# A decoder trunk in one kernel: attention scores and values as products of high and low parts, a stacked rotary part, and buffers laid out anew

## What is computed

```python
# layer A: differential attention, 8 heads, two maps a head, head dim 128, values 256 wide
s1 = einsum(qa, k1) * 128**-0.5;  s2 = einsum(qb, k2) * 128**-0.5
a  = causal_softmax(s1) - lam * causal_softmax(s2)
o  = rms_norm(a @ v, subln_g) * (1 - lam_init)
x += o @ w_o
x += square(relu(rms_norm(x) @ w_up)) @ w_down            # d_ff = 8192
# shared latents and layer B: 16 heads, 128 plain + 64 rotary columns, values 128 wide
kv = rms_norm(rms_norm(x) @ w_dkv[:, :512]) @ w_ukv ;  k_rope = rope(rms_norm(x) @ w_dkv[:, 512:])
q  = rms_norm(rms_norm(x) @ w_dq) @ w_uq
s  = (einsum(q_nope, k_nope) + einsum(rope(q_rope), k_rope)) * 192**-0.5
x += (causal_softmax(s) @ v) @ w_o ;  x += square(relu(rms_norm(x) @ w_up)) @ w_down
return rms_norm(x, final_norm_g)
```

## Time and profile before

| | us |
|---|---|
| median of 3 runs | 2063.35 |
| the profiled execution | 2063.65 |
| its span, first to last instruction | 2061.9 |
| TensorE matmuls busy | 2051.7 (100%) |
| TensorE weight loads busy | 1761.2 (85%) |
| VectorE busy | 1194.4 (58%) |
| ScalarE busy | 989.3 (48%) |
| GpSimd busy | 10.1 (0%) |

### The profile page before, as it was taken

One profiled execution on the slowest core, in us unless ns is written; L12 is line 12 of the kernel. 1 busy time (PEld: TensorE's weight loads), 2 busy tenths in 40 slices (PEclk: granted clock), 3 DMA queues, 4 the chain that ended last, 5 costly groups with the idle time before them and its releaser, 6 DMA issues.

```text
span 2061.9 us, 28683 instructions
## 1 busy us (share of the span) xinstructions
PE 2051.7 (100%) x10470; PEld 1761.2 (85%) x10470; DVE 1194.4 (58%) x1474; ACT 989.3 (48%) x1360; POOL 10.1 (0%) x22
## 2 busy tenths in 40 slices
PE   9999999999999999999999999999999999999998
PEld 7888888888888888888888998888888888888887
DVE  7655555565556556555655666566556556655655
ACT  7554555444345334434446665544434434434443
POOL 0000000000000000000000000000000000000000
PEclk9999999999999999999999999999999999999999
DMA  7655545665665665556555444575666556656653
GB/s 278 239 164 169 177 161 166 190 196 186 194 193 176 207 187 184 202 183 190 196 184 164 136 131 146 187 218 184 198 190 183 200 186 183 202 187 181 203 186 120
DMA packets 261129, 381.76 MB, mean 185 GB/s; under 512 B 8785, under 2 KB 145233, under 8 KB 260945
## 3 DMA queue, kind: packets, MB, share of 16 engines
q1 hardware_dynamic: 260352, 378.90, 57.3%
q10 hardware_dynamic: 720, 2.10, 0.3%
HBM read 378.87 MB, written 2.10 MB: 185 GB/s over the span
## 4 chain that ended last, share of the span: by engine, by line
PE 84%; issue 15%; DVE 0%; POOL 0%; ACT 0%; POOLq 0%; DVEq 0%
PE acc L470 23%; PE acc L441 15%; PE acc L443 15%; PE acc L442 15%; PE acc L480 12%; PE side L505 1%; PE side L785 0%; PE side L784 0%; PE acc L751 0%; PE acc L759 0%; PE acc L760 0%; PE acc L761 0%; PE acc L752 0%; PE acc L753 0%; PE side L795 0%
## 5 line engine op out<-in xcount | busy, mean ns | idle before, releaser
L1289 DVE TENSOR_TENSOR wlo<-raw,whi 128x1024 fp32r<-128x1024 f32 (+1 forms) x700 | 840.3, 1213 | 663.5 <-ACT whi L879 661.7
L879 ACT ACTIVATE whi<-raw 128x1024 fp32r<-128x1024 f32 (+1 forms) x700 | 726.2, 1051 | 727.8 <-PE acc L443 479.4
L441 PE MATMUL acc<-whi,opB 128*128 128x512 f32 x1264 | 493.4, 390 | 0.0
L443 PE MATMUL acc<-whi,opB 128*128 128x512 f32 x1264 | 491.9, 389 | 0.0
L442 PE MATMUL acc<-wlo,opB 128*128 128x512 f32 x1264 | 491.8, 389 | 0.0
L470 PE MATMUL acc<-opA,whi 128*128 128x512 f32 x2048 | 478.2, 390 | 0.0
L470 PEld LDWEIGHTS acc<-opA,whi 128*128 128x128 f32 x2048 | 380.3, 188 | 76.2
L443 PEld LDWEIGHTS acc<-whi,opB 128*128 128x128 f32 x1264 | 237.2, 188 | 49.5
L441 PEld LDWEIGHTS acc<-whi,opB 128*128 128x128 f32 x1264 | 237.3, 188 | 48.7
L442 PEld LDWEIGHTS acc<-wlo,opB 128*128 128x128 f32 x1264 | 237.3, 188 | 48.7
L480 PEld LDWEIGHTS acc<-opA,wlo 128*128 128x128 f32 x2048 | 254.2, 192 | 5.0
(11 more groups left out here) (203 smaller groups left out, 986.0 us busy)
## 6 DMA issues: line engine op xcount, KB each, us to landing
raw<-in_w_up SPq DMA_DIRECT2D x128, 1024.0 KB, 5.8
raw<-in_w_down SPq DMA_DIRECT2D x128, 1024.0 KB, 5.0
raw<-in_a_w_qkv SPq DMA_DIRECT2D x44, 1024.0 KB, 5.1
raw<-in_a_w_o SPq DMA_DIRECT2D x16, 1024.0 KB, 5.0
raw<-in_b_w_o SPq DMA_DIRECT2D x16, 1024.0 KB, 5.0
raw<-in_w_ukv SPq DMA_DIRECT2D x8, 1024.0 KB, 5.5
raw<-in_b_w_uq SPq DMA_DIRECT2D x8, 576.0 KB, 4.0
raw<-in_w_dkv SPq DMA_DIRECT2D x4, 1024.0 KB, 5.1
```

What stands on the lines that cost most here:

```text
L441: mm(o, a_hi, w_hi, start=first and c == 0, stop=False)
L443: done = mm(o, a_lo, w_hi, start=False, stop=last and c == chunks - 1)
L879: done = fn(whi[:, place:place + ch, 0:n], raw[:, r, c0:c0 + ch, 0:n], ACT.Copy)
L1289: done = tt_(wlo[:, place:place + ch, 0:n], raw[:, r, c0:c0 + ch, 0:n], whi[:, place:place + ch, 0:n].bitcast(F32), ALU.subtract)
```

## The change

- q, k, v of the first attention, and q and k of the second, are kept as high and low parts (`qk`, `v_hl`, type fp32r). ScalarE copies the high part out of PSUM as before, VectorE writes the low part (new: `qk_lo`, `v_lo`, `mla_q_lo`, `mla_k_lo`). The transposed softmax weights of the first attention too (`attnT_hl`, `da_attnT_lo`).
- Scores of both attentions and values of the first are three fp32r products instead of one fp32 product. In the second attention the rotary part is one tile per head with the high rows in one half of the partitions and the low rows in the other, times k's high rows, stacked twice, and times its low rows: two products. Its values stay fp32.
- In urgent blocks TensorE does halves 0 and 1 together, and 6 and 7, tile by tile (`two_halves`); it counts both as done at the end.
- ScalarE drains v of the second attention one half earlier, and k's accumulator is freed by VectorE's low part.
- The sum of squares of x in the first K block, some table work and the asides at the second projection move by one half.
- Buffers: x's first columns lie in `xs`, whose own load waits for them; the gains have their own DMA; `up_sb`, `v_mla` and others share `o_sb`; the squares use `junk`; the final gain comes in two halves into `stage` and `prob`, and the output is written in place in `xs`.

```diff
-        krz = sb("krz", [P, 2, SEQ])
+        qk = sb("qk", [P, 2, 2, 4, SEQ], F32R)
+        v_hl = sb("v_hl", [P, 2, TT, NB], F32R)
+        attnT_hl = sb("attnT_hl", [P, 2, 2, KEYS], F32R)
...
+            def two_halves(b, hf, s, op, first=False, last=False, uses=0):
+                for t in range(TT):
+                    for h in range(2):
+                        pe.wait_ge(lo_ready, 8 * b + hf + h + 1)
+                        for c in range(2):
+                            start, end = first and h == 0 and c == 0, last and h == 1 and c == 1
+                            if start:
+                                wait_bank(s, uses, t)
...
+                            done = mm(o, a_lo, whi[:, place, :], start=False, stop=end)
+                            if end and t == 0:
+                                done.then_inc(bank0_done, 1)
+                done.then_inc(pe_halves, 2)
...
             def da_scores(p, first=False):
-                pe.wait_ge(qkT_ready, 4 * p + 4)
+                pe.wait_ge(qkT_lo, 4 * p + 4)
...
-                    mm(side[m][:, 0:P], qT[:, m, 0:P], kT[:, m, 0:P], start=True, stop=True)
-                    mm(side[m][:, P:KEYS], qT[:, m, P:SEQ], kT[:, m, :], start=True,
-                       stop=True).then_inc(scores_done, 1)
+                    for rows, keys, cols in ((slice(0, P), slice(0, P), slice(0, P)),
+                                             (slice(P, SEQ), slice(0, SEQ), slice(P, KEYS))):
+                        o = side[m][:, cols]
+                        mm(o, q_hi[:, m, rows], k_hi[:, m, keys], start=True, stop=False)
+                        mm(o, q_hi[:, m, rows], k_lo[:, m, keys], start=False, stop=False)
+                        done = mm(o, q_lo[:, m, rows], k_hi[:, m, keys], start=False, stop=True)
+                    done.then_inc(scores_done, 1)
...
+                            mm(o, a_hi[:, keys], v_hl[:, 0, kt, cols], start=k == 0, stop=False)
+                            mm(o, a_hi[:, keys], v_hl[:, 1, kt, cols], start=False, stop=False)
+                            done = mm(o, a_lo[:, keys], v_hl[:, 0, kt, cols], start=False, stop=k == len(parts) - 1)
...
-                block_tok(b + 1, 1, p, opA, urgent=True, aside={1: x_sum_squares, 7: lambda: transpose_qk(2 * p, 0)} if first else {
+                block_tok(b + 1, 1, p, opA, urgent=True, aside={2: x_sum_squares, 7: lambda: transpose_qk(2 * p, 0)} if first else {
...
             def mla_scores(p):
-                pe.wait_ge(drained[1], 2 * (U_MLA[1] + p) + 1)
-                pe.wait_ge(qkT_ready, 2 * DA_PAIRS * 2 + 2 * p + 2)
+                pe.wait_ge(drained[1], 2 * (U_MLA[1] + p) + 2)
+                pe.wait_ge(qkT_lo, 4 * DA_PAIRS + 2 * p + 2)
...
+                        mm(o, q_hi[:, h, rows], k_hi[:, h, keys], start=True, stop=False)
+                        mm(o, q_hi[:, h, rows], k_lo[:, h, keys], start=False, stop=False)
+                        mm(o, q_lo[:, h, rows], k_hi[:, h, keys], start=False, stop=False)
+                        mm(o, qr[:, h, rows], kr_hi[:, keys], start=False, stop=False)
+                        done = mm(o, qr[:, h, rows], kr_lo[:, keys], start=False, stop=True)
...
+            def drain_v(b):
+                act.wait_ge(bank0_done, b + 1)
+                for t in range(TT):
+                    if t:
+                        used(b)
+                    fn(v_hl[:, 0, t, :], acc[0][:, t, :], ACT.Copy, scale=rs[:, 0, t:t + 1]).then_inc(v_hi, 1)
...
                 body(b + 2, asides)
-                drain_qkv(b + 2, 0, kv_sb[:, 0])
+                drain_v(b + 2)
                 exps(4 * p, (2, 3), (0, 1, 2, 3), DA_SCALE)
...
             def mla_drain_kv(b, hf, par):
+                act.wait_ge(pe_halves, 8 * b + hf)
+                fn(v_mla[:, par], acc[1][:, 1, :].rearrange("p (t n) -> p t n", t=TT), ACT.Copy).then_inc(drained[1], 1)
                 act.wait_ge(pe_halves, 8 * b + hf + 1)
-                fn(kT[:, 0:2, :], acc[1][:, 0, :].rearrange("p (h t) -> p h t", h=2), ACT.Copy).then_inc(drained[1], 1)
-                fn(kv_sb[:, par, :, 0:2 * VDIM], acc[1][:, 1, :].rearrange("p (t n) -> p t n", t=TT),
-                   ACT.Copy).then_inc(drained[1], 1)
+                fn(k_hi[:, 0:2, :], acc[1][:, 0, :].rearrange("p (h t) -> p h t", h=2), ACT.Copy).then_inc(k_ready, 1)
...
+            def v_lo(p):
+                for t in range(TT):
+                    dve.wait_ge(v_hi, TT * p + t + 1)
+                    stt(out=v_hl[:, 1, t, :], in0=acc[0][:, t, :], scalar=rs[:, 0, t:t + 1],
+                        in1=v_hl[:, 0, t, :].bitcast(F32), op0=ALU.mult, op1=ALU.subtract).then_inc(drained[0], 1)
...
+            def mla_k_lo(p):
+                dve.wait_ge(k_ready, p + 1)
+                tt_(k_lo[:, 0:2, :], acc[1][:, 0, :].rearrange("p (h t) -> p h t", h=2), k_hi[:, 0:2, :].bitcast(F32),
+                    ALU.subtract).then_inc(drained[1], 1)
...
                 split(nb, h0 + 1, nxt)
                 if prev2:
                     mla_lo(p - 2)
+                mla_k_lo(p)
                 rope_mla(p)
```

More of the change, by code:

```diff
@@ L344, in _ @@
             qkv(0, True)
+            sp.wait_ge(x_sums, 5)
             for j in range(JB):
@@ L425, in wait_bank, with half_tok @@
                     pe.wait_ge(drained[s], 2 * uses - 1 + bank)
-            def half_tok(b, hf, s, op, n=NB, chunks=2, first=False, last=False, uses=0, urgent=False):
+            def half_tok(b, hf, s, op, n=NB, chunks=2, first=False, last=False, uses=0, by_tile=False):
                 pe.wait_ge(lo_ready, 8 * b + hf + 1)
@@ L432, in half_tok @@
                 order = [(c, t) for c in range(chunks) for t in range(TT)]
-                if urgent and (first or last):
+                if by_tile:
                     order = [(c, t) for t in range(TT) for c in range(chunks)]
@@ L443, in half_tok @@
                     done = mm(o, a_lo, w_hi, start=False, stop=last and c == chunks - 1)
-                    if urgent and last and t == 0 and c == chunks - 1:
-                        done.then_inc(bank0_done, 1)
                 done.then_inc(pe_halves, 1)
+            def two_halves(b, hf, s, op, first=False, last=False, uses=0):
[6 more added lines that the diff above has]
+                                wait_bank(s, uses, t)
+                            a_hi, a_lo = (op[2 * h + c][i][:, P * t:P * t + P] for i in range(2))
+                            place = 2 * ((hf + h) % 4) + c
+                            o = acc[s][:, t, :]
+                            mm(o, a_hi, whi[:, place, :], start=start, stop=False)
+                            mm(o, a_hi, wlo[:, place, :], start=False, stop=False)
+                            done = mm(o, a_lo, whi[:, place, :], start=False, stop=end)
+                            if end and t == 0:
+                                done.then_inc(bank0_done, 1)
+                done.then_inc(pe_halves, 2)
             def chunks_of(buf, c0, n=2):
@@ L454, in block_tok @@
                         ready(hf)
-                    half_tok(b, hf, s, chunks_of(buf, 2 * hf), n, first=hf == 0, last=hf == 7, uses=uses,
-                             urgent=urgent)
+                    if urgent and hf in (0, 6):
+                        two_halves(b, hf, s, chunks_of(buf, 2 * hf, 4), first=hf == 0, last=hf == 6, uses=uses)
+                    elif not (urgent and hf in (1, 7)):
+                        half_tok(b, hf, s, chunks_of(buf, 2 * hf), n, first=hf == 0, last=hf == 7, uses=uses)
                     if aside and hf in aside:
@@ L1199, in mla_copies @@
                 act.wait_ge(qkT_done, 2 * DA_PAIRS + 2 * p + 1)
-                fn(qT[:, 0:2, :], side[0][:].rearrange("p (h t) -> p h t", h=2), ACT.Copy).then_inc(qkT_ready, 1)
+                fn(q_hi[:, 0:2, :], side[0][:].rearrange("p (h t) -> p h t", h=2), ACT.Copy).then_inc(qkT_ready, 1)
                 act.wait_ge(qkT_done, 2 * DA_PAIRS + 2 * p + 2)
-                fn(qT[:, 2, :], side[2][:, 0:SEQ], ACT.Copy).then_inc(qkT_ready, 1)
+                for h in range(2):
+                    half = slice(ROPE * h, ROPE * h + ROPE)
+                    done = fn(qr[half, h, :], side[2][half, 0:SEQ], ACT.Copy)
+                done.then_inc(qkT_ready, 1)
             def mla_exps(p):
@@ L1594, in up_block, with with_norm_weight @@
                     square_up(q, j, 1)
+                def with_norm_weight(j):
+                    dve.wait_ge(g_out_in, 32)
+                    for t in range(TT):
+                        dve.wait_ge(xsq, 2 * (V_MLP1 + j) + t + 1)
+                        y = xs[:, t, NB * j:NB * j + NB]
+                        tt_(y, y, g_columns(j), ALU.mult).then_inc(xg_ready, 1)
                 def add_scaled(b, s, prior, cols):
@@ L1682, in mla_weights, with mla_q_lo @@
                             ALU.mult).then_inc(attn_ready, 1)
+            def mla_q_lo(p):
+                dve.wait_ge(qkT_ready, 4 * DA_PAIRS + 2 * p + 1)
```

(11 more changed lines are left out.)

183 lines of the change are left out of this document (103 added, 80 removed).

## The result

| | before | after |
|---|---|---|
| median | 2063.55 us (2062.99 to 2063.88) | 2087.12 us (2085.57 to 2089.54) |
| ratio | | 1.0116, 95% interval 1.0098 to 1.0133 |
| profiled execution, span | 2063.65, 2061.9 | 2087.31, 2085.2 |
| mean granted clock | 0.999 | 0.997 |
| PE, DVE, ACT busy | 2051.7, 1194.4, 989.3 | 2055.6, 1230.3, 991.4 |

The account below looks back on a forecast made before the run. TensorE, busy throughout, was taken as the bound: matmul pitches plus its waits. Terms -3.5 + 10.1 + 0.65 + 11.2 + 1.5 + 0.45 + 0.1 = +20.5 us on 2063.65 gave 2084 us, range 2072 to 2096.

Parts of the forecast that it names:

- Products, -3.5: Both attentions: fp32r products replacing fp32 ones in scores and the first's values save 3.5 us of TensorE time together.
- A: Rival, chance 0.13: a 128-column fp32r product runs no faster than today's fp32 one, 0.22 us; 2093.5 us.
- C: Rival, chance 0.07: the weight load hides and a 128-column product costs 0.067 us; 3.9 us less, 2080 us.
- Ends of V blocks, +10.1: First attention, three V-to-Q boundaries: TensorE waits 3.37 us each for V's low part, queued behind the next split.
- B: Rival, chance 0.08: the 3.4 us waits make the clock fall, 2.4 us each, three times 7.3; 2091 us.
- Second attention's pairs, +11.2: Each pair's first product waits for k's low part, queued on VectorE: 1.48 us for pairs 2 to 7, less earlier pairs.
- First K block, +1.5: TensorE waits 0.9 us at half 1 and 2.4 at half 7; the sum-of-squares wait of 1.26 goes; net +1.5 us.
- Output projection +0.65: After the last V block, exponentials start 1.5 us later, so weights reach the first output projection late: +0.65 us.
- Gains +0.45: Kernel start: one more DMA, for the gains alone, issued ahead of x's first columns: +0.45 us.
- Latents +0.1: k's rotary part gets a low row on VectorE at a point where TensorE waits already: +0.1 us.
- D: Rival, chance 0.10: the waits don't arise; only the products' -3.5 and the sum of squares' 1.26 us remain; 2059.3 us.
- theory 3: Theory behind the follow-up experiments: the products themselves gain 3.5 us, which a version without the waits would show.

Follow-up runs that it names:

- e1: Changed kernel with V's drain (ScalarE) and V's low part (VectorE) ahead of the next block's split of half 2; 2072.21 us.
- e2: Changed kernel with halves 0 and 1, 6 and 7 of the first attention's blocks done one by one again, as before the change; 2074.08 us.
- e11: Changed kernel with 24 unused identity transposes on TensorE ahead of the second, third and fourth Q blocks, filling its wait; 2083.91 us.
- e10: As e9, and halves 0, 1, 6 and 7 of the first Q and K blocks done one by one; 2062.47 us.
- e9: As e4, plus rotation tables later in the first K block, and q's drain, rotation and the transposed-weights copy earlier in second-attention pairs; 2062.51 us.
- e3: Changed kernel; second attention: output's high part and k, v drains ahead of ScalarE's split, k's low part directly behind the softmax weights on VectorE; 2083.03 us.
- e5: Changed kernel with V's low part ahead of the split's low part on VectorE only, ScalarE's order as in the change; 2087.41 us.
- e4: Changed kernel with the reorderings of e1 and e3 together, the change's products kept; 2065.84 us.

## Why the prediction came out as it did

The forecast was 2084.0, measured 2087.1. The mechanism was right in its main part: TensorE's pitches plus waits set the time, and the two large kinds of wait came where the prediction put them. One term, the clock, was put at nothing and measured 4.8 us. The terms, against the stages and rows:

- **Products, -3.5.** Right in the pitches: scores of the first attention 2.76 us a pair (2.77 forecast), of the second 2.30 (2.31), values -0.45 a pair (the second K block; the prediction's own 2.61 - 2.16 is 0.45, too, though it wrote 0.43). No measured time shows the 3.5 us by themselves. Rivals A and C fall: the 128-column product takes 0.11 us, neither 0.22 nor 0.067. The figure of about 81 ns in the Trainium skill ("TensorE: Matmul & The Clock Gate", Back-to-back issue gap) isn't reached here; its weight load of 107 ns for 128 columns (LDWEIGHTS) is close to the 0.11 us of the rows.
- **Ends of V blocks, +10.1.** 3.29, 3.23 and 3.23 us: 9.75. e1 and e2 show the two causes, the place in the queues and the joined halves; with either taken away the long wait is gone.
- **The clock, priced at 0 in the forecast.** This is the step that failed. I held B for a rival with a chance of 0.08; it came true beside the forecast, not instead of it, with 1.6 us each and not 2.4 (the stretch is 3.4 us long, the start's was longer): +4.8. I took "the longest wait today is 1.1 us with full clock" as evidence against, though, as the forecast itself noted, it said nothing of 3.4 us; the earlier trace rows spoke for it. e1 and e11 show it.
- **Second attention's pairs, +11.2.** Seven waits of 1.34 (six at pairs, one at the output projection's start), 0.63 behind pair 0, 0.61 at pair 1's transposes, where the kernel before had lost 0.41 already, and 0.10 at each second matmul behind a wait. The forecast had 1.48 for pairs 2 to 7, 1.7 for pair 1 and 0.6 for pair 0. With the shorter scores the stretch grew by 8.44, where 11.2 - 7 x 0.3 = 9.1 was forecast.
- **First K block, +1.5.** (The prediction's own terms, 0.9 + 2.4 - 1.26 - 0.35, give 1.7.) Measured -0.05: half 1 did not wait at all, because the whole block started 1.1 us later, and the forecast had not carried even its own 0.45 of the gains into that start; half 7 waited 1.56, not 2.4; the 1.26 and the 0.35 went as said. Unforeseen: the first Q block grew by 0.80, of which 0.40 is a wait at its joined last halves (24.78) and the rest gaps of about 0.1 us among its first matmuls.
- **Output projection +0.65**: 0.31 and 0.21 us at the transposes, 0.52. **Gains +0.45**: 0.34, but the first matmul starts anywhere from 5.42 to 5.70 us in the eleven profiles with this load order, against 5.35 before, so this one execution doesn't size the term. **Latents +0.1**: none seen; the one late start inside pair 0 even shrank, from 0.34 to 0.18. **At nothing**: the output in place, the shared buffers, the later load; the 818.3 us between the attentions and all behind the second output projection's first block are unchanged to 0.02 us.

Without the clock the stages sum to 23.2 - 4.8 = 18.4 us (forecast 20.5), so that the forecast came within 3.1 us is partly luck: the overestimates of the waits and the missing clock cancelled in part. D is refuted by the waits; but its 2059.3 (its two terms give 2063.35 - 3.5 - 1.26 = 2058.6) asked what the products are worth alone. e10 comes to 2062.5: 0.9 us faster than the kernel before beside it, within what this measurement can tell from nothing. So theory 3 stands by the pitches alone. The second attention's 2.4 us did not come with any order tried here: its pairs are at 14.12 us in e9, as before.

## What to carry over

Before an operation's second reader (a low part) is added, list for each buffer who frees it last and what stands ahead of that reader in its engine's queue; here the order of the same instructions was worth 24.6 us (the changed kernel against e10, the low clock included) and the arithmetic 3.5 by its pitches. When a wait of TensorE grows past those the profile has at full clock, price the clock too, as an addition to the forecast. And a cheaper product pays only until the chain beside it becomes the limit: look for gaps of hundredths that no list of waits shows.

## What the runs showed of the hardware

- The granted clock fell to 0.5 for one stretch of 3.4 us behind waits of TensorE: behind waits of 3.2 to 3.3 us each time one was profiled (3 of 3 in the changed kernel, 3 of 3 in e3), of 2.7 us 2 of 3 times (e5), of 2.0 to 2.1 us in the profiles of e3, e4 and e11, but by the executions' times probably not in all of e4's. It did not fall behind 1.56 us in the changed kernel nor behind 1.61 in e5. It fell once behind 1.35 us (e5, at 1183), which came 0.74 us after a wait of 0.61; the other waits of 1.35 us there, and the seven in each of the changed kernel, e1, e2 and e11, had full clock. The stretch began from 0.2 us before to 0.6 us behind the first matmul after the wait, and 1.1 and 1.5 us behind it in e4 and e3. So the length of the single wait doesn't decide it alone: 2.73 us once left the clock full, and 0.61 + 1.35 us lowered it. I can't name what does.
- Three fp32r products of a 128-column operand take 3 x 0.11 us, an fp32 one of the same shape 0.22, so at 128 columns the split loses; at 256 it wins, 3 x 0.12 against 0.44. The 0.11 is also the pitch of the one-column matmuls; that it is the weight load's is inferred from this.
- Half 7 of the first K block waits 1.56 us in the changed kernel and 0.8 to 2.1 us in other versions, whose queues have the same order there. The reason is when a piece of the weights lands. ScalarE's split for this block's first half waits for that DMA, and from there ScalarE and VectorE run through the tables and splits without a pause that differs. In the changed kernel and in e3:

```profile
25.10 1.06 ACT L916 ACTIVATE whi<-raw 128x1024 fp32r<-128x1024 f32 x1 [0.68 <-DMA raw<-in_a_w_qkv]
47.48 1.23 DVE L1337 TENSOR_TENSOR wlo<-raw,whi 128x1024 fp32r<-128x1024 f32 x1 [2.37 <-ACT whi L916]
```
```profile
26.06 1.06 ACT L916 ACTIVATE whi<-raw 128x1024 fp32r<-128x1024 f32 x1 [1.32 <-DMA raw<-in_a_w_qkv]
48.46 1.23 DVE L1337 TENSOR_TENSOR wlo<-raw,whi 128x1024 fp32r<-128x1024 f32 x1 [2.37 <-ACT whi L916]
```

In the seven profiles with the tables in their old place (the changed kernel, e1 to e5 and e11) the split starts between 25.06 and 26.29, and the low part of half 7 ends 23.6 us behind it every time. What TensorE waits is the difference to its own arrival, which varies with the first pieces' landing as well. So the longer wait in e3, e4 and e11, and the low clock behind it, aren't effects of those edits.
